# Attention steps with casts, splits, rotations and epilogues placed earlier in two queues

## The reference

```python
oa = diff_attention(qa, ka, va, lam)
yb = u * mixed.reshape(B, S, B_WIDTH) * jax.nn.silu(bz)
o_p, lse_p = dilated_window_attention(qc, kc, vc, window, dil)
merged = jnp.einsum('bsnd,nbsd->bsd', gates, pb)
return x + jnp.einsum('bsd,de->bse', merged, w_out)
```

```python
out_a = _causal_softmax_blocks(fq, fk, fv, HEAD_DIM ** -0.5, cum)       # FOX
out_b = _mla(cq, ckv, kr, g_q, g_kv, w_uq, w_ukv, cos, sin)             # MLA
out_c = _stick_breaking_blocks(sq, sk, sv)                              # SB
out_d = _swa_sink_alibi(wq, wk, wv, sinks, slopes)                      # SWA
```

## Time and profile before

| | us |
|---|---|
| median of 3 runs | 2515.79 (2511.89 to 2516.4) |
| profiled execution | 2514.11 |
| its span | 2512.3 |
| TensorE busy | 2454.8 (98%) |
| VectorE busy | 1242.2 (49%) |
| ScalarE busy | 945.7 (38%) |
| mean granted clock of TensorE | 0.997 |

### The profile page before, as it was taken

How to read it: one execution, slowest core, us unless ns; L and a number is a source line. 1 busy time by engine, 2 the same in 40 slices (tenths; PEclk the granted TensorE clock), 3 DMA queues, 4 the chain that set the end, 5 groups by cost and what they waited for, 6 DMA issues and landing times.

```text
span 2512.3 us, 30092 instructions
## 1 busy us (share of the span) xinstructions
PE 2454.8 (98%) x11932; PEld 1958.6 (78%) x11932; DVE 1242.2 (49%) x2019; ACT 945.7 (38%) x1765; POOL 0.2 (0%) x4
## 2 busy tenths in 40 slices
PE   8999999999999999999999999999999999999998
PEld 6888778887888778887766688888886667888887
DVE  6577554345577653344554453333355445433334
ACT  5345432223345442223546542212245554322222
POOL 0000000000000000000000000000000000000000
PEclk9999999999999999999999999999999999999999
DMA  4333223331343223333211133333322112333332
GB/s 160 103 89 89 81 75 99 96 116 60 100 108 89 80 62 113 100 95 106 56 54 51 51 103 101 93 101 93 117 66 69 43 51 76 101 97 96 100 94 92
DMA packets 65643, 221.46 MB, mean 88 GB/s; under 512 B 9056, under 2 KB 9696, under 8 KB 64736
## 3 DMA queue, kind: packets, MB, share of 16 engines
q1 hardware_dynamic: 65360, 219.28, 29.2%
q10 hardware_dynamic: 144, 0.26, 0.0%
HBM read 205.88 MB, written 2.10 MB: 83 GB/s over the span
## 4 chain that ended last, share of the span: by engine, by line
PE 90%; DVE 5%; ACT 3%; issue 1%; DMA 1%; SPq 0%; DVEq 0%; ACTq 0%
PE bank L452 26%; PE bank L454 25%; PE bank L453 25%; PE bank L1008 2%; PE bank L1608 1%; DVE w_lo L860 1%; PE bank L1649 1%; PE bank L995 1%; DMA raw_w<-w_dram 1%; PE bank L978 1%; PE bank L975 1%; PE bank L1672 1%; PE bank L1633 1%; PE bank L392 1%; ACT w_hi L852 1%
## 5 line engine op out<-in xcount | busy, mean ns | idle before, releaser
L452 PE MATMUL bank<-h_hi,w_hi 128*128 128x512 f32 x2000 | 802.8, 401 | 4.6 <-ACT ks L1825 3.4
L454 PE MATMUL bank<-h_lo,w_hi 128*128 128x512 f32 x2000 | 781.4, 391 | 0.0
L453 PE MATMUL bank<-h_hi,w_lo 128*128 128x512 f32 x2000 | 780.0, 390 | 0.0
L860 DVE TENSOR_TENSOR w_lo<-raw_w,w_hi 128x1024 fp32r<-128x1024 f32 x360 | 433.6, 1222 | 223.5 <-ACT w_hi L852 219.1
L852 ACT ACTIVATE w_hi<-raw_w 128x1024 fp32r<-128x1024 f32 x360 | 377.8, 1058 | 318.8 <-DMA raw_w<-w_dram 318.8
L452 PEld LDWEIGHTS bank<-h_hi,w_hi 128*128 128x128 f32 x2000 | 376.2, 188 | 95.6 <-issue 22.5
L454 PEld LDWEIGHTS bank<-h_lo,w_hi 128*128 128x128 f32 x2000 | 375.8, 188 | 81.0
L453 PEld LDWEIGHTS bank<-h_hi,w_lo 128*128 128x128 f32 x2000 | 376.6, 188 | 72.0 <-issue 0.2
L452 PE MATMUL bank<-w_hi,act_hi 128*128 128x512 f32 x480 | 189.4, 395 | 2.6 <-DVE w_lo L860 2.6
L454 PE MATMUL bank<-w_lo,act_hi 128*128 128x512 f32 x480 | 187.0, 390 | 0.0
L453 PE MATMUL bank<-w_hi,act_lo 128*128 128x512 f32 x480 | 187.0, 389 | 0.0
(11 more groups left out here) (308 smaller groups left out, 2860.8 us busy)
## 6 DMA issues: line engine op xcount, KB each, us to landing
raw_w<-w_dram SPq DMA_DIRECT2D x360, 512.0 KB, 3.6
extra_raw<-w_dram SPq DMA_DIRECT2D x10, 512.0 KB, 5.1
ln_row<-row_dram SPq DMA_DIRECT2D x4, 1024.0 KB, 5.8
x<-x_dram SPq DMA_DIRECT2D x4, 512.0 KB, 6.9
rowp<-row_dram SPq DMA_DIRECT2D x2, 1024.0 KB, 10.8
rot_t<-raw_t SPq DMA_DIRECT2D x128, 16.0 KB
act_hi<-q_lo SPq DMA_DIRECT2D x16, 128.0 KB, 2.3
act_lo<-act_lo SPq DMA_DIRECT2D x16, 128.0 KB, 2.3
```

Of the source, the lines that this page charges most:

```text
L452: nc.tensor.matmul(dst, lh, rh, start=start, stop=False)
L453: nc.tensor.matmul(dst, ll, rh, start=False, stop=False)
L454: return nc.tensor.matmul(dst, lh, rl, start=False, stop=stop)
L860: nc.vector.tensor_tensor(lo_of(u), raw_of(u), hi_of(u).bitcast(F32), ALU.subtract) \
```

## The change

Only the order within ScalarE's and VectorE's queues changes, in the attention steps of both blocks. No instruction is added or taken away, and TensorE's and SP's programs stay.

In block 1 ScalarE does the cast, the tile copy and the V copy of the step before ahead of the exponentials; `pT_copy` follows the exponentials at once, and `output_rstd` follows that. VectorE does the split, rotation and epilogue between the maxima and `normalise`.

In block 2 ScalarE casts for the tiles that ended in the step before ahead of the exponentials, unless an `rstd` is made in this step; in that case these casts stay where they were, at the step's end. VectorE splits for the same tiles right behind the maxima (SB: behind `sb_softplus_sum`), and `normalise` comes behind the latent splits, rotations and group norms. `add_squares("cq")` and `gate_sums` come behind `normalise`.

```diff
 # ScalarE, block 1
+                    before = steps_back(a, qb, 1)
+                    if before and fill_of(*before):
+                        tile, f = fill_of(*before)
+                        cast_to(act, n0 + head_unit(tile, f) + 3)
+                        if tile == "z":
+                            z_tanh(f)
+                        else:
+                            raw_copy(tile, f)
+                    if LATE1.get(before, ("", 0))[0] == "v":
+                        v_copy(LATE1[before][1])
                     softmax_exp(a, qb, 0)
                     softmax_exp(a, qb, 1)
...
                     if before:
...
+                        pT_copy(*before)
                         if LATE1.get(before, ("", 0))[0] == "sum":
                             output_rstd(LATE1[before][1])
-                        pT_copy(*before)
 # VectorE, block 1
+                    if (a, qb) == (0, 0):
+                        split_to(dve, n0 + B1_HEADS + 6)
+                    elif fill_of(*before):
+                        split_to(dve, n0 + head_unit(*fill_of(*before)) + 3)
                     if before in ROTATE1:
                         rotate(*ROTATE1[before])
-                    normalise(a, qb)
                     if qb == 0 and 2 <= a < N_A + 2:
                         epilogue(a - 2)
...
-                    if (a, qb) == (0, 0):
-                        split_to(dve, n0 + B1_HEADS + 6)
-                    elif fill_of(*before):
-                        split_to(dve, n0 + head_unit(*fill_of(*before)) + 3)
+                    normalise(a, qb)
 # ScalarE, block 2
+            def casts_of(tiles):
+                for name in tiles:
+                    next_cast(name)
...
                 if late in V_TILES:
                     v_copy(late)
-                elif late == "cq":
+                if late == "cq":
                     rstd("cq", sz[0], 2 * P)
                 elif late == "ckv":
                     rstd("ckv", z_t, P)
                 elif late[:1] == "e":
                     rstd(late, nrm, 4 * HD)
+                else:
+                    casts_of(ended)
...
-                for name in (*ended, *ENDS[step, 0]):
-                    next_cast(name)
+                casts_of((*ended, *ENDS[step, 0]))
 # VectorE, block 2
                     row_max(a, qb, 0)
                     row_max(a, qb, 1)
-                    normalise(a, qb)
-                if late == "cq":
-                    add_squares("cq", *sz)
+                for name in ended:
+                    next_split(name)
...
-                if "gates" in ENDS.get((step - 2, 1), []):
-                    gate_sums()
                 for tile, steps in ((0, 1), (1, 2)):
                     squared = LATE.get(step - steps, "")
                     if squared[:1] == "e":
                         group_norm(int(squared[1]) - 1 + tile)
-                for name in (*ended, *ENDS[step, 0]):
+                if not is_sb(step):
+                    normalise(a, qb)
+                if late == "cq":
+                    add_squares("cq", *sz)
+                if "gates" in ENDS.get((step - 2, 1), []):
+                    gate_sums()
+                for name in ENDS[step, 0]:
                     next_split(name)
```

More of the change, by code:

```diff
@@ L1225, in scalar_block1 @@
                 for qb in range(NB):
+                    before = steps_back(a, qb, 1)
[8 more added lines that the diff above has]
+                        v_copy(LATE1[before][1])
                     softmax_exp(a, qb, 0)
                     softmax_exp(a, qb, 1)
-                    before = steps_back(a, qb, 1)
                     if before:
[L1230 to L1239, removed]
+                        pT_copy(*before)
                         if LATE1.get(before, ("", 0))[0] == "sum":
                             output_rstd(LATE1[before][1])
-                        pT_copy(*before)
                     if qb == 1 and 1 <= a <= N_A:
```

## The result

| | before | after |
|---|---|---|
| median, us (range, runs) | 2514.72 (2511.89 to 2516.4, 4) | 2499.49 (2499.24 to 2500.68, 4) |
| profiled execution, its span | 2514.11, 2512.3 | 2499.24, 2497.5 |

A forecast was written before the change was run, and what follows sets the result against it. TensorE was taken as the bound, busy 2454.8 of 2512.3 us. Block 1's end -4.2, block 2's order -2.3 and the clock -3.4 sum to -9.9, giving 2504.2; with 1.7 for the median, 2506; range 2501 to 2514.

The forecast's parts named there:

- clock term: Block 2's attention: both halved-clock stretches a layer go, one new comes at step 27; -1.7 us a layer, -3.4 in all.
- step 27: Block 2, head 6, query block 3: late cast blocks normalisation, TensorE stalls 3.2 us; +1.3 a layer after recovery.
- old falls: Block 2: two drops a layer to half clock, behind waits of 2.30 and 1.19 us, to vanish; about 1.7 each.
- step 6: Block 2: a split done sooner brings the maxima and the copy into ks earlier; -0.45 us a layer.
- (a): End of block 1's attention: copy of transposed probabilities follows exponentials at once, removing a weighted-V wait; -1.1 us a layer.
- (b): End of block 1's attention: early tanh(z) removes VectorE's 1.25 us idle before silu; gain 1.0 us a layer.
- Step 3: Block 2: VectorE's split waits for a late cast, delaying normalisation and the transposes; +1.5 us a layer.
- step 8: Block 2: rotation of qr moves ahead of normalisation, so the scores' wait for it goes; -2.3 us a layer.
- Step 13: Block 2: group norm fills an earlier wait, so the scores' wait for exponentials goes; -1.2 us a layer.
- 1 (clock gives nothing): Block 2's attention: as many clock falls as before; -6.5 us in all, 2509.3; chance 0.18.
- 3 (old falls stay): Block 2: old falls belong to small-matmul stretches and stay, step 27 adds one; -3.1 us in all, 2512.7; chance 0.11.
- 2 (no new fall): Block 2: no new clock fall comes in step 27; -13.3 us in all, 2502.5; chance 0.10.

## Why the prediction was right in direction and too small

**The step that failed** is the last half of the clock term, with the tail of step 27: "put one new one behind the 3.2 us stall of step 27: net -1.7 a layer", beside "+1.3" for the stall. The fall came where it was put, and was priced as the old ones, whose stretches TensorE paces. Here VectorE paces: maxima, exponentials and normalisation of steps 28 to 31 take their time at either clock. At half clock TensorE spends 1.0 us more on eight transposes and one set of scores (1.37 and 1.65 against 1.09 and 0.92), which it would otherwise spend waiting. With the clock kept whole only 0.42 us came back in layer 1 and 1.35 in layer 2, not 1.7. The order itself costs 3.07 less what comes back: from the transposes to step 31's weighted V it is 14.21 before (1416.62 to 1430.83) and 12.03 with the clock whole, so +0.9 and not +1.3. Together +3.6 for both layers where +6.0 stood: 2.4 of the 4.9 us by which the sum was short. The old falls were priced nearly right, at 1.7 for a measured 1.6.

Of the rest, 0.9 is the weighted V in step 6. I wrote that "kr's rotation gains nothing" from moving. Its result z_t frees `raw_t`; ScalarE's next copy into `raw_t` starts at 1259.32 before and at 1253.72 after, 1.0 earlier against TensorE, whose own starts moved 4.59 at the step before, and the copy of transposed probabilities stands right behind it in the queue. The run with late rotations takes just this gain back. I had not looked for what is queued behind the copy. Another 0.7 was won before the first changed instruction and is no effect of the edit. Block 1's end brought 1.0 more, because (a) gave 1.56 a layer and not 1.1: beside the wait of 1.12 ahead of the twelve weighted V, a second one among them went, so that they take 0.88 and not 1.25. The small terms left over make 0.1 the other way. Last, I added 1.7 for the median lying above the profiled execution. After the change it lies only 0.25 above: the executions of the kernel before are spread over 2511.9 to 2516.4, those of the kernel after over 1.4 us. 4.9 and 1.45 make the 6.5, with the rounding of the forecast from 2505.9 to 2506.

**Point by point.** In block 1's filled steps no transposes of L995 wait, as said; the steps drift by 0.3 us in all, in pieces too small for a row. Of its end, (b) gave the 1.0 of its row and (a) more than its own, and ScalarE's part alone gives it all. Step 3's +1.5 came out as said, and step 27's stall of 3.2 is 3.07; the chain cast, split, normalisation was read rightly both times, and early casts or late splits take it away. Step 6's copy gave 0.52 for 0.45, step 8's wait 2.35 for 2.3, and the row exchange was in time. Step 13 with both old falls gave 4.8 a layer for 4.6: the order 1.6 for 1.2, since the scores themselves take 0.70 and not 1.04, and the falls 3.2 for 3.4. The old falls belong to their waits, as the idle matmuls show. The Trainium skill (TensorE: Matmul & The Clock Gate, HAM oscillation) lets long idle gaps throttle the engine: the trace agrees at 3.07 us, and shows falls behind 1.19 us as well.

**Rivals.** 1 (clock gives nothing) and 3 (old falls stay) are refuted: in its attention stages the profiled execution after has two falls for the four before, none of them at the old places, and the idle matmuls show what the old ones cost. 2 (no new fall) gives the nearest number, 2502.5, for another reason: the new falls came and cost 1.8 in all. 4 and 5: step 27 recovered 1.8 of its 3.1 in layer 1 and 0.8 in layer 2, and the exchange was not late. 6: block 1's waits fell by 4.4.

## What to carry to other kernels

In a queue worked in order, an instruction that waits for another engine blocks all that stands behind it: before moving one ahead of the chain that TensorE needs, move what it waits for first, in every case of the code and not only in the common branch. A clock fall or a slow matmul costs its full price only where TensorE sets the pace, so look at what it would wait for in that stretch before pricing it. When a wait goes, look also for the queue behind the copies that it released.

## What the runs showed of the hardware

- Falls of the clock follow idle time but not its length alone. In the profiled executions they stood behind 2.30, 1.19 and 3.07 us of waiting, and behind 1.12 or 1.13 at block 1's end (block 2's part alone, and the kernel before with idle matmuls); not behind 1.69 (kernel before) nor 1.32 (after). The same wait had a fall in one place and none in another. The 1.12 had none in the kernel before. Step 8's wait of 2.2 to 2.3 had none in the first layer with ScalarE's order alone in block 1, and none in the second with late rotations. With step 11's old order the 1.19 wait stood in both layers, and only the first had a fall.
- A fall of 3.4 us to half clock cost 1.6 us at steps 8 and 13, where TensorE sets the pace, and 0.42 at step 27 of the first layer, where VectorE does.
- On the kernel before, filling two waits a layer with matmuls whose results are dropped kept the clock whole there and won 6.5 us without shortening any wait for data.
- The same kernel runs at more than one level: the version with late rotations took 2495.17 and 2495.45 at a mean clock of 0.998, 2499.82 and 2500.99 at 0.996. 0.002 of 2498 us is 5.0 us, about the distance between the levels, as far as a clock given to 0.001 can tell. Why a fall comes in one execution and not in another stays open.
